# Both feed-forward blocks of a two-layer encoder by Strassen's seven quadrant products, in two phases with spilled tiles

## The reference, cut to what matters

```python
def conv_gated_ffn(h, w_up, conv_w, conv_b, w_down):        # D_MODEL 1024, D_FF 2816
    a = h @ w_up                                            # (512, 5632) per sequence
    a = depthwise_conv_width_3(a, conv_w) + conv_b          # along the tokens
    gate, val = jnp.split(a, 2, axis=-1)
    return (jax.nn.silu(gate) * val) @ w_down               # (512, 1024)
...
    x = x + conv_gated_ffn(rmsnorm(x, ffn_norm_g[i]), ...)
```

## Time and profile before

| | |
|---|---|
| time, median of 3 runs | 2155.87 us (2154.67 to 2159.37) |
| span of the profiled execution, first to last instruction | 2153.3 us |
| own time of the profiled execution | not listed apart; the median stands 2.6 us above the span |
| first feed-forward block | about 423 to 1148 us of the span |
| second feed-forward block | about 1431 to 2150 us |

### The profile page before, as it was taken

One profiled execution on the slowest core, in us unless ns is written; L12 is line 12 of the kernel. 1 busy time (PEld: TensorE's weight loads), 2 busy tenths in 40 slices (PEclk: granted clock), 3 DMA queues, 4 the chain that ended last, 5 costly groups with the idle time before them and its releaser, 6 DMA issues.

```text
span 2153.3 us, 27074 instructions
## 1 busy us (share of the span) xinstructions
PE 2123.6 (99%) x9728; PEld 1751.1 (81%) x9728; DVE 1306.5 (61%) x1745; ACT 749.4 (35%) x1032; POOL 104.0 (5%) x84
## 2 busy tenths in 40 slices
PE   7999999999999999999999999999999999999999
PEld 6988777888888888888887888888888888888887
DVE  6398874576565665565657244556665566665655
ACT  5334686632222222222225432333232222222221
POOL 2022000300000000000003000110000000000000
PEclk9999899999999999999999999999999999999999
DMA  5210000131111111111103211121111111111112
GB/s 179 64 49 29 26 16 8 53 106 44 36 38 58 58 58 39 39 39 58 58 0 108 88 32 37 50 79 59 59 49 39 41 47 58 58 49 37 31 39 78
DMA packets 146627, 112.84 MB, mean 52 GB/s; under 512 B 3856, under 2 KB 133392, under 8 KB 146576
## 3 DMA queue, kind: packets, MB, share of 16 engines
q1 hardware_dynamic: 146432, 111.95, 16.8%
q10 hardware_dynamic: 144, 0.21, 0.0%
HBM read 107.95 MB, written 4.19 MB: 52 GB/s over the span
## 4 chain that ended last, share of the span: by engine, by line
PE 96%; DVE 2%; ACT 1%; issue 0%; DMA 0%; SPq 0%; ACTq 0%; DVEq 0%
PE bank L426 28%; PE bank L428 28%; PE bank L427 28%; PE bank L485 2%; PE bank L486 2%; PE bank L487 2%; PE bank L541 2%; PE bank L569 1%; PE bank L552 1%; PE bank L543 1%; PE bank L686 0%; DVE act2l L1057 0%; DVE act1l L1057 0%; DVE sumsq L1071 0%; DVE x L1248 0%
## 5 line engine op out<-in xcount | busy, mean ns | idle before, releaser
L931 ACT ACTIVATE conv_out<-conv_in,vectors 128x512 f32<-128x512 f32 x176 | 143.7, 816 | 510.5 <-DVE conv_in L1272 464.0
L426 PE MATMUL bank<-hidh,dwh 128*128 128x512 f32 x704 | 274.6, 390 | 3.0 <-DVE x L1248 2.8
L428 PE MATMUL bank<-hidh,dwl 128*128 128x512 f32 x704 | 273.9, 389 | 0.0
L427 PE MATMUL bank<-hidl,dwh 128*128 128x512 f32 x704 | 273.9, 389 | 0.0
L1272 DVE TENSOR_TENSOR conv_in<-bank,rstd 128x512 f32<-128x512 f32 x176 | 121.4, 690 | 222.2 <-PE bank L428 222.1
L1248 DVE TENSOR_TENSOR x<-bank,x 128x512 f32<-128x512 f32 x352 | 231.2, 685 | 41.3 <-PE bank L428 41.3
L1277 DVE SCALAR_TENSOR_TENSOR conv_out<-conv_in,vectors,conv_out 128x512 f32<-128x512 f32 x176 | 132.1, 750 | 197.4 <-ACT conv_out L931 197.4
L426 PE MATMUL bank<-act2h,uwh 128*128 128x512 f32 x528 | 206.2, 391 | 0.0
L426 PE MATMUL bank<-act1h,uwh 128*128 128x512 f32 x528 | 206.2, 391 | 0.0
L428 PE MATMUL bank<-act2h,uwl 128*128 128x512 f32 x528 | 205.4, 389 | 0.0
L428 PE MATMUL bank<-act1h,uwl 128*128 128x512 f32 x528 | 205.4, 389 | 0.0
(11 more groups left out here) (182 smaller groups left out, 3928.8 us busy)
## 6 DMA issues: line engine op xcount, KB each, us to landing
uws<-w_up SPq DMA_DIRECT2D x88, 512.0 KB, 3.8
dws<-w_down SPq DMA_DIRECT2D x22, 1024.0 KB, 4.9
gws<-w_in SPq DMA_DIRECT2D x32, 256.0 KB, 2.5
vws<-w_qkv SPq DMA_DIRECT2D x32, 192.0 KB, 2.4
qws<-w_qkv SPq DMA_DIRECT2D x12, 512.0 KB, 3.9
x<-xT SPq DMA_DIRECT2D x8, 512.0 KB, 7.4
mws<-w_out SPq DMA_DIRECT2D x8, 512.0 KB, 3.9
yT<-x SPq DMA_DIRECT2D x16, 256.0 KB, 2.0
```

The source lines that it names most:

```text
L426: mm(out, wh, ah, start=first, stop=False)
L427: mm(out, wh, al, start=False, stop=False)
L428: return mm(out, wl, ah, start=False, stop=last)
L931: A(m["y"][:, t % 2], m["a"][:, t % 2, 1:S + 1], ACT.Identity, scale=col(tap), bias=col(offset)) \
```

## The change

In both feed-forward blocks each matrix product is cut into two by two quadrants and made by Strassen's method in Winograd's form, with seven products of quadrants where eight are needed otherwise. The quadrants are: weights by halves of the contraction and by gate/value (up) or neighbouring output tiles (down); activations by halves of the contraction and by the two sequences.

A *job* is seven products (`P1, P2, P6, P5, P7, P3, P4` in this order), each of `half_k` (4, in the last chunk 3) times 3 matmuls. A layer has 22 up jobs (one for each 128 hidden rows), and then 12 down jobs (three chunks of the hidden layer, `CHUNKS`, times four pairs of output tiles). In numbers: 22 x 84 + 8 x 84 + 4 x 63 = 2772 matmuls a layer.

What goes with it:

- Four weight sums for each job on POOL (`s_sum`), of 512 fp32 elements in each partition, and the split of seven weight operands for each product, ACT `hi(n)` and DVE `part(n)`, in a ring of four.
- Two up jobs share a pair of hidden tiles; from its four gated tiles POOL makes four differences (`h_diffs`: one after an even job, three after an odd one). The seven tiles of the pair, operands of the later down products, go to device memory (`keep_job`) and come back by chunks (`refill`, 1 MB for each of 7 operands, 2 KB rows), to be split again (`refilled`: four operands on DVE, P6, P7, P4 on POOL, 2048 elements each).
- Half of `x` goes to device memory during the up jobs, since its place holds the gated tiles.
- The norm is put into the split: before the first product a matmul with diagonal matrices spreads the inverse root over the partitions, and `first_jobs` multiplies `x` by gain and root on DVE and forms the seven activation operands.
- Within a job three PSUM banks hold the products, some accumulating onto others; ACT copies three of them out between products (`copy_t1`, `copy_u2`, `copy_p5`), DVE adds three pairs (`c11`, `c22`, `c12`).
- All of it is straight code, without hardware loops.

The core of the diff on PE, DVE, ACT and POOL:

```diff
+ORDER = FIRST + tuple((j, q) for j in range(2, NJOB) for q in range(NOP))
+RING = 4
...
+            def product(layer, n):
+                j, o = ORDER[n]
+                    if o == P6:
+                        pe.wait_ge(cp_t1, layer * NUP + j + 1)
+                    if o == P7:
+                        pe.wait_ge(cp_u2, layer * NUP + j + 1)
+                    if o == P3:
+                        pe.wait_ge(cp_p5, layer * NUP + j + 1)
+                    if o == P4:
+                        pe.wait_ge(c_add, cj + 2)
...
+                pe.wait_ge(sp_lo, layer * NPROD + n + 1)
+                for k in range(h):
+                    mm(b, wh, bh[o][:, k], start=OPENS[o] and k == 0, ...)
+                    mm(b, wh, bl[o][:, k], ...)
+                    last = mm(b, wl, bh[o][:, k], ...)
...
+                def up_job(j):                      # ACT
+                    gate(j - 1, 1)
+                    mid(j - 1, 3)
+                    hi(n0 + 3)
+                    copy_t1(j)
+                    hi(n0 + 4)
+                    mid(j, 0)
+                    hi(n0 + 5)
+                    copy_u2(j)
+                    hi(n0 + 6)
+                    gate(j, 0)
+                    copy_p5(j)
...
+                def up_job(j):                      # DVE
+                    taps(j - 1, 2)
+                    gated_hidden(j - 1, 1)
+                    part(n0 + 3)
+                    taps(j - 1, 3)
+                    gated_hidden(j - 1, 0)
+                    part(n0 + 4)
+                    c11(j)
+                    part(n0 + 5)
+                    taps(j, 0)
...
+                def up_job(j):                      # POOL
+                    s_sum(j + 1, S1)
+                    s_sum(j + 1, S2)
+                    h_diffs(j - 1)
+                    s_sum(j + 1, S4)
+                    s_sum(j + 1, S3)
...
+                def down_job(j):                    # POOL
+                    if q == 0:
+                        refilled(chunk, P7)
+                        refilled(chunk, P4)
+                    if j == NUP:
+                        h_diffs(j - 1)
+                    if j + 1 < NJOB:
+                        s_sums(j + 1)
+                    if q == 3 and chunk + 1 < len(CHUNKS):
+                        refilled(chunk + 1, P6)
```

1077 lines of the change are left out of this document (721 added, 356 removed).

## The result

The changed kernel takes **2270.95 us** (median of four runs, 2267.29 to 2275.58) against 2157.62 us for the kernel before beside it: a ratio of 1.053, interval 1.0505 to 1.055. I had forecast 2102 us, faster, in a range that ended at 2185. The profiled execution has a span of 2273.8 us, 120.5 us above that of before.

A forecast was written before the change was run, and what follows sets the result against it. The prediction took the kernel as PE-bound in the changed stage: 2153.3 - 179.4 + 60 + 26 + 34 + 6 = 2099.9 us of span, 2102 us as median, with a range of 2030 to 2185 us.

The forecast's parts named there:

- Term 1, products: Feed-forward products: 3168 matmuls a layer become 2772, two layers save 792 at 0.2265 us, -179.4 us.
- The reading of the door: DVE instructions with two SBUF inputs and POOL hold one access in turn; a blocked DVE instruction loses 0.44 or 1.08 us.
- the walk: Step-by-step pass through the engines' instruction lists, for block starts and the even-running up jobs; also those jobs' stage itself.
- Term 2, start: Start of each feed-forward block: waiting for the norm, then DVE behind; 30 us a layer, +60 us for two.
- First product at 435: At a block's start, the first product begins at 435 us, after attention's last matmul at 423.0 and the norm's steps.
- Between them I take 30: At a block's start, 30 us a layer, chosen between 16 (POOL blocks nothing) and 40 (every hold in full).
- Term 3, up jobs: 20 even-running up jobs a layer: DVE meeting POOL lengthens a job past 19.03 us by 0.65 us, +26 us.
- halfway between the two prices: Up jobs: 0.65 us a job (19.7 us), between meetings with POOL costing 0.44 us and 1.05 us each.
- Term 4, borders: Three borders a layer where operands are refilled, 7 MB each: 17 us a layer, between 3 and 30, +34 us.
- Term 5, clock: PE's granted clock falls after idle spells: 3 us for each block's start, +6 us.
- the door decides, slower: Rival, chance 0.25: DVE's list bounds the up jobs, long POOL splits cost in full; 214 us against 179.4, about 2190 us.
- a period over 21 us: Sign named beforehand: an up job's period above 21 us would mean the forecast is wrong in sign.

The follow-up runs named there:

- e2: Changed kernel with POOL's weight sums of up jobs 2 to 21 and most gated-tile differences cut to one column, the rest left out: 2198.12 us.
- e1: Changed kernel with POOL's long instructions (1536 or 2048 elements) cut into three or four of 512, same work and order: 2226.95 us.
- e7: Changed kernel with e1, e3 and e4 together, plus POOL's four first weight sums of each block moved behind the last square adds: 2190.61 us.
- e18: e15 with the sum C11 moved earlier on VectorE and a second tile for the gate's first half in odd jobs: 2111.83 us, ratio 0.9804.
- e3: Changed kernel with SyncE's queue reordered so that refills at the borders stand ahead of weight loads: 2243.09 us.
- e15: e9 with ScalarE's weight high halves ahead of waiting refill copies and VectorE's refilled low halves earlier at the borders: 2141.47 us, ratio 0.9936.
- e9: e7 with weights' high halves also written to PSUM by ScalarE from job 2 on, and VectorE's low halves subtracting that copy: 2152.76 us.
- e10: e7 with POOL's weight sums of the down jobs cut to one column, the rest left out: 2182.99 us.
- e11: e7 with 54 unused matmuls added at each block's start, where PE stands: 2190.82 us.
- e4: Changed kernel with ScalarE's copy of P5 out of PSUM ahead of the gate's activation in each up job: 2270.73 us, ratio 1.0524.

## Why the prediction was wrong

- **Term 1, products, -179.4 us:** right. 5544 product matmuls, and where POOL is nearly silent (e2) the period is 19.03 us.
- **The reading of the door:** right that there is one, and nearly right in its length. I took POOL's hold as 1.05 us for 512 elements and 4.2 for 2048; beside long POOL instructions DVE's short ones took 4.35 to 5.03 us, 3.7 to 4.3 more than alone. What went wrong is how much of it I counted: the full hold stood only in the ceilings, and the sum took 30 of 40 us at a start, the middle of 3 and 30 at the borders and half of the price in the walk. All three came out at the ceiling or over it (the walk at 1.71 us a job where the ceiling was 1.7). Cutting the long instructions (five at each block's start, where I had counted six, and nine at its borders) is worth 44 us in e1.
- **Term 2, start, +60 (bounds 32 and 80):** measured 103. Two steps failed. "First product at 435", 12 us behind attention, is 21 and 24: the spreading takes 3.78 us for 1.2, the column sums 3.57 for nearly nothing, the first low half 4.64 for 0.7, and POOL's four weight sums, put at no cost, are worth 2.5 to 3 (e7). And "Between them I take 30": behind the first product the walk with every hold in full gave 71.7 us to the end of P1 of job 2, and both blocks measured 71.9. So the start cost 50 and 53 us, the ceiling of 40 and the 9 and 12 us ahead of the first product. That the walk came out so closely may be in part luck: e1, with the holds in pieces, gave back only 2.7 us behind the first product and 3 ahead of it.
- **Term 3, up jobs, +26 (bounds 0 and 68):** measured 65. The walk with 1.05 a meeting gave 20.2 and 21.2 us and the measured periods are 20.0 and 21.3, 20.74 in the mean: the mechanism and even PE's first wait (P3 for `cp_p5`) were right. The failed step is "halfway between the two prices"; nothing in the rows spoke for the half. What the walk left out is that its chain runs through one tile from job to job, which e18 shows as a lever.
- **Term 4, borders, +34 (bounds 6 and 60):** measured 128, some 3 of it the walk's price in the two jobs 21. This is the step that was mis-modelled. It assumed that a refill starts when its product frees it; in SyncE's queue the first stood 13.7 us behind a weight load (e3, 28 us). It left out the order on ACT and DVE, where high halves of weights stood behind copies that waited for transfers (e15, 11 us), and it counted only half of the long POOL holds (e1, about 32 us of its 44 fall here). These overlap: e7 gives 53 of 62 us. The PSUM copies gave 7 more a block (e9 against e7). What stays after all of these is 22 to 26 us a block, of which e10 puts 4 on POOL's sums, in e7's order. The amount of 7 MB a border is a candidate for the rest: the first border's seven refills take 24.1 us from the first issue to the last landing in the changed kernel and 25.6 in e15, near the 24 forecast, and I made no run with less.
- **Term 5, clock, +6:** as a term of its own it is not shown. The clock is low in these stretches (0.73 from 423 to 441 us in e7). e11 raised it in two windows of the start, the column sums fell from 2.77 to 1.84 us, and the block's third job was no earlier in the first block and 2 us in the second, with matmuls of its own in the way. At the borders it wasn't tried.
- **The rival on the other side**, "the door decides, slower", at 2190 us, is what happened, with its sign and its places. Its price of 214 us was built of ceilings; the bills came to 296, and most of the difference is the borders (60 against 128), where more than the door was at work. The sign of being wrong that I had named, a period over 21 us, did not come: the mean was 20.74, and the borders made the rest. A chance of 0.25 was too low for a case whose order of DVE's instructions showed a two-input instruction at hand nearly always.

## What to carry to other kernels

An instruction that holds a shared resource can cost its neighbour its whole length, and where the neighbour always has work at hand, plan with the ceiling and not with a half. Cut long ones in pieces where their own engine has the time; here POOL took 7.2 us in pieces for 4.67 whole, and the kernel still gained 44. Move one operand of VectorE's instruction to PSUM where a bank is idle; here 4 us a job of ScalarE's idle time bought it, and 38 us. And when no engine is full and each waits for others, count the round trip, with its buffers: three sensible reorderings, each aimed at the wait that the trace named, made it longer, and one more tile of 2 KB a partition, with one of them, took 30 us off the best version without it.

## What was not expected of the hardware

- A 512-element instruction of DVE took 4.35 to 5.03 us beside one POOL instruction of 4.5 to 4.84 us, and with POOL's work cut into 512-element pieces the long low half of DVE took 2.28 to 3.37 us (e9).
- ScalarE writes fp32r halves of 512 elements into PSUM in 0.59 us (e9), and VectorE subtracts with the fp32r bits read there as fp32: 0.684 us beside a busy POOL.
- One refill of 1 MB takes 11.6 us to land in the median where seven are issued together with weights, against 4.9 us for 1 MB before.
- The last matmul of attention, in code that no run changed, began at 420.2 to 430.5 us in the profiled executions, up to 10 us of a single span. It goes with the granted clock from 230 to 290 us: 0.89 to 0.91 in the twelve executions in which it began by 423.0 us, 0.86 in the six from 426.2 to 427.5 us, 0.80 in e4 (429.2) and 0.74 in the kernel after (430.5). Why the clock differs there between executions is not shown.
